# Silu in one function, squares and a rounded copy behind it, and norm sums in two parts, in the convolution of a fused two-layer kernel

## What is computed

```python
gqkv = jax.nn.silu(causal_conv(gqkv, conv_w)).astype(f32)
gq, gk, gv = jnp.split(gqkv, [GDN_HEADS * GDN_DK, 2 * GDN_HEADS * GDN_DK], axis=-1)
gq = l2_normalize(gq.reshape(b, s, GDN_HEADS, GDN_DK)) * (GDN_DK ** -0.5)
gk = l2_normalize(gk.reshape(b, s, GDN_HEADS, GDN_DK))
gv = gv.reshape(b, s, GDN_HEADS, GDN_DV)
...
def l2_normalize(t):
    return t * lax.rsqrt(jnp.sum(t * t, axis=-1, keepdims=True) + 1e-6)
```

## Time and profile before

| | |
|---|---|
| median of 3 runs | 2767.71 us (2766.85 to 2773.09) |
| profiled execution | 2766.82 us, its span 2765.1 us |
| TensorE clock granted | 1.00 of full over the span |
| TensorE matmuls, weight loads | 2746.5 us, 2443.9 us busy |
| VectorE, ScalarE, GpSimd | 1907.3, 1353.2, 59.4 us busy |
| stage of the delta rule beside convolutions | about 1055 to 1580 us |

### The profile page before, as it was taken

One profiled execution on the slowest core, in us unless ns is written; L12 is line 12 of the kernel. 1 busy time (PEld: TensorE's weight loads), 2 busy tenths in 40 slices (PEclk: granted clock), 3 DMA queues, 4 the chain that ended last, 5 costly groups with the idle time before them and its releaser, 6 DMA issues.

```text
span 2765.1 us, 39573 instructions
## 1 busy us (share of the span) xinstructions
PE 2746.5 (99%) x16256; PEld 2443.9 (88%) x16256; DVE 1907.3 (69%) x2553; ACT 1353.2 (49%) x1741; POOL 59.4 (2%) x103
## 2 busy tenths in 40 slices
PE   9999999999999999999999999999999999999998
PEld 8899888888888889999999988888888888888887
DVE  7655567778866657888888885566666655666556
ACT  5434654447444436656565643543354443444444
POOL 0000210000000000000000000000000000000000
PEclk9999999999999999999999999999999999999999
DMA  7444445465555454444444445554355455555554
GB/s 273 183 193 158 151 169 197 184 251 184 208 178 211 180 186 168 153 153 153 151 154 151 169 168 212 183 191 163 141 206 197 184 192 204 202 194 191 195 193 152
DMA packets 72852, 506.64 MB, mean 183 GB/s; under 512 B 8384, under 2 KB 8512, under 8 KB 12896
## 3 DMA queue, kind: packets, MB, share of 16 engines
q1 hardware_dynamic: 71136, 497.77, 48.6%
q0 software_dynamic: 1104, 5.90, 0.6%
q10 hardware_dynamic: 432, 0.45, 0.0%
HBM read 499.89 MB, written 2.10 MB: 182 GB/s over the span
## 4 chain that ended last, share of the span: by engine, by line
PE 95%; DVE 3%; ACT 1%; issue 1%; DMA 1%; SPq 0%; DVEq 0%; ACTq 0%
PE double L1399 88%; PE bank L1399 6%; PE bank L1402 1%; DVE wlo L2117 1%; ACT whi L1775 0%; DVE AA L2123 0%; DMA vec<-in_vec 0%; DMA raw<-in_wall 0%; DVE Tn L2625 0%; DVE gz L2117 0%; ACT tmp L1952 0%; DVE ob L2123 0%; DVE acc L2117 0%; ACT L1952 0%; SPq L2920 0%
## 5 line engine op out<-in xcount | busy, mean ns | idle before, releaser
L1399 PE MATMUL double<-AA,whi 128*128 128x512 f32 (+3 forms) x5776 | 1617.0, 348 | 3.3 <-DVE wlo L2117 3.2
L1775 ACT ACTIVATE whi<-raw 128x1024 fp32r<-128x1024 f32 x926 | 926.1, 1050 | 785.2 <-PE double L1399 735.1
L1399 PE MATMUL double<-AA,wlo 128*128 128x256 f32 (+1 forms) x4624 | 1274.9, 276 | 0.0
L2117 DVE TENSOR_TENSOR wlo<-raw,whi 128x1024 fp32r<-128x1024 f32 (+1 forms) x934 | 1100.4, 1214 | 191.8 <-ACT whi L1775 188.7
L1399 PEld LDWEIGHTS double<-AA,whi 128*128 128x128 f32 (+1 forms) x5776 | 1003.9, 188 | 147.3 <-DVE wlo L2117 5.0
L1399 PEld LDWEIGHTS double<-AA,wlo 128*128 128x128 f32 x4624 | 866.7, 187 | 1.0
L1399 PE MATMUL double<-whi,AA 128*128 128x512 f32 x1536 | 481.0, 388 | 0.0
L1399 PEld LDWEIGHTS double<-whi,AA 128*128 128x128 f32 x1536 | 288.1, 188 | 52.7 <-issue 1.9
L1399 PE MATMUL double<-whi,BB 128*128 128x512 f32 x1024 | 309.5, 382 | 0.0
L1399 PE MATMUL double<-wlo,AA 128*128 128x512 f32 x768 | 293.4, 382 | 0.0
L1399 PEld LDWEIGHTS double<-whi,BB 128*128 128x128 f32 x1024 | 191.8, 187 | 33.8
(11 more groups left out here) (334 smaller groups left out, 1688.1 us busy)
## 6 DMA issues: line engine op xcount, KB each, us to landing
raw<-in_wall SPq DMA_DIRECT2D x462, 1024.0 KB, 4.8
raw<-in_wall SPq DMA_DIRECT2D x9, 256.0 KB, 6.4
X<-in_xT SPq DMA_DIRECT2D x1, 2048.0 KB, 11.3
Mm<-in_memT POOLq DMA_DIRECT2D x1, 2048.0 KB, 15.5
tmp<-rqk POOLq DMA_DIRECT2D x16, 128.0 KB, 2.2
mblk<-in_memT SPq DMA_DIRECT2D x8, 256.0 KB, 4.5
dec<-in_dec POOLq DMA_DIRECT2D x1, 1536.0 KB, 8.6
hs<-in_hsT SPq DMA_DIRECT2D x4, 272.0 KB, 5.6
```

The lines of the kernel that those rows point to most:

```text
L1399: return q.matmul(out, lhsT, rhs, start=start, stop=stop, skip_group_check=True)
L1775: q.activation(hi_of(j)[:, c], raw[j % RAW][:, c], ACT.Copy).then_inc(S("w_hi"), 1)
L2117: return q.tensor_tensor(out, a, b, o)
```

## The change

For q, k and v ScalarE applies Silu to `cacc` and writes `qkv[n]` itself; the product on VectorE goes away. For q and k two more functions follow at once on ScalarE: the square into the temporary buffer, and a copy of it rounded to fp32r into `cacc_r`, which lies where `cacc` lies. VectorE then subtracts the rounded copy from the square (stage `cvl`, in the place of `cvq`), and the sum over partitions is two fp32r matmuls with a matrix of ones rounded to fp32r: one of the high part, one of the low. The next convolution's first tap waits for these two matmuls, since they read the place of `cacc`; after v's it waits for Silu. v's convolution takes no temporary buffer. `ones_r` is written once, by ScalarE, at the start of the stage.

```diff
 g_conv:
         r = add("cv1", (h, n), v=up("cnv_vec", 4))
+        if n == 2:
+            r = add("cvs", (h, n), a=up("cnv_act"))
+            P.cacc = P.at["got", ("v", h)] = ("cnv_act", r["a"])
+            tasks.append(g_gdn(h))
+            return
         t, tf = tmp.take()
         tmp.held.add(t)
-        r = add("cvs", (h, n), t=t, tf=tf, a=up("cnv_act"))
-        if n == 2:
-            tasks.append(g_gdn(h))
-            yield
-            r = add("cvv", h, t=t, z=up("cnv_vec"))
-            tmp.free(t, "cnv_vec", r["z"])
-            P.cacc = ("cnv_vec", r["z"])
-            P.at["got", ("v", h)] = ("cnv_vec", r["z"])
-            return
+        r = add("cvs", (h, n), t=t, tf=tf, a=up("cnv_act", 3))
         yield
         if h:
             lo_to(done["lo"] + 1)
-        r = add("cvq", (h, n), t=t, z=up("cnv_vec"), a=up("cnv_act"))
-        P.cacc = ("cnv_vec", r["z"])
+        r = add("cvl", (h, n), t=t, lo=up("cnv_vec"))
         yield
         yield
         b, bf = side.take()
         r = add("cvn", (h, n), t=t, b=b, bf=bf, full=up("cnv_pe"), a=up("cnv_act", 2))
         side.free(b, "cnv_act", r["a"] - 1)
+        P.cacc = ("cnv_pe", r["full"])
...
+    cacc_r = place(kpos[1], [P_, 512], F32R, name="cacc_r")
+    ones_r = place(con_off + 4 * CON["room"][0], [P_, P_], F32R, name="ones_r")
...
 TensorE, s_cvn:
-            q.wait_ge(S("cnv_act"), at["cvq", key]["a"])
-            mm_group(bank[r["b"]][:, :], C("ones"), tmps[r["t"]][:, :]).then_inc(S("cnv_pe"), 1)
+            q.wait_ge(S("ones_r"), 1)
+            q.wait_ge(S("cnv_act"), at["cvs", key]["a"])
+            mm_group(bank[r["b"]][:, :], ones_r[:, :], cacc_r[:, :], start=True, stop=False)
+            q.wait_ge(S("cnv_vec"), at["cvl", key]["lo"])
+            mm_group(bank[r["b"]][:, :], ones_r[:, :], tmps_r[r["t"]][:, :], start=False, stop=True).then_inc(S("cnv_pe"), 1)
...
 ScalarE:
+        def s_begin_gdn(_, r):
+            q.wait_ge(S("ret_m"), RET_END)
+            q.activation(ones_r[:, :], C("ones"), ACT.Copy).then_inc(S("ones_r"), 1)
+
         def s_cvs(key, r):
-            q.preload_act_table_set("sigmoid_and_others")
-            free(r["tf"])
+            h, n = key
+            q.preload_act_table_set("silu_and_others")
+            if h:
+                q.wait_ge(S("gdn_pe"), at["g_vb" if n == 2 else "g_x", h - 1]["p"])
             q.wait_ge(S("cnv_vec"), at["cv1", key]["v"])
-            q.activation(tmps[r["t"]][:, :], f2(cacc), ACT.Sigmoid).then_inc(S("cnv_act"), 1)
-
-        def s_cvq(key, r):
-            q.wait_ge(S("cnv_vec"), r["z"])
-            s = tmps[r["t"]][:, :]
-            q.activation(s, f2(qkv[key[1]]), ACT.Square).then_inc(S("cnv_act"), 1)
+            q.activation(f2(qkv[n]), f2(cacc), ACT.Silu).then_inc(S("cnv_act"), 1)
+            if n < 2:
+                s = tmps[r["t"]][:, :]
+                free(r["tf"])
+                q.wait_ge(S("cnv_act"), r["a"] - 2)
+                q.activation(s, f2(qkv[n]), ACT.Square).then_inc(S("cnv_act"), 1)
+                q.wait_ge(S("cnv_act"), r["a"] - 1)
+                q.activation(cacc_r[:, :], s, ACT.Copy).then_inc(S("cnv_act"), 1)
...
 VectorE:
-        def s_cvq(key, r):
-            h, n = key
-            if h:
-                q.wait_ge(S("gdn_pe"), at["g_x", h - 1]["p"])
+        def s_cvl(key, r):
             q.wait_ge(S("cnv_act"), at["cvs", key]["a"])
-            tt(f2(qkv[n]), f2(cacc), tmps[r["t"]][:, :], ALU.mult).then_inc(S("cnv_vec"), 1)
+            tt(tmps_r[r["t"]][:, :], tmps[r["t"]][:, :], cacc_r[:, :].bitcast(F32), ALU.subtract).then_inc(S("cnv_vec"), 1)
```

More of the change, by code:

```diff
@@ L105 @@
 for _name, _n in (("ident", 128), ("ones", 128), ("nones", 128), ("ntri", 128), ("upto", 128), ("beyond", 128),
-                  ("strict", 64), ("eye", 64), ("below", 64), ("m2", 32), ("m4", 32), ("m8", 32),
+                  ("strict", 64), ("room", 128), ("eye", 64), ("below", 64), ("m2", 32), ("m4", 32), ("m8", 32),
                   ("m16", 32), ("m32", 32), ("invf", 1), ("eps6", 1), ("eps5", 1), ("eps12", 1), ("sgn", 1), ("mhalf", 4)):
@@ L120, in constants @@
         "upto": p <= f, "beyond": p > f, "strict": g < r, "below": -1.0 * ((g == r) | ((r % 2 == 1) & (g == r - 1))),
-        "eye": p % 64 == f[:, 0:64], "mhalf": np.full((P, 4), -0.5), "sgn": np.where(np.arange(P) < 64, -1.0, 1.0)[:, None],
+        "eye": p % 64 == f[:, 0:64], "room": np.zeros((P, P)), "mhalf": np.full((P, 4), -0.5), "sgn": np.where(np.arange(P) < 64, -1.0, 1.0)[:, None],
         "invf": (1.0 / (np.float32(10000.0) ** (np.arange(0, 128, 2, dtype=np.float32) / np.float32(128))))[
@@ L2100, in scalar_program @@
                "a7": gained("a7", lambda k: V("norm_ffn_g_2", k)), "trig": s_trig, "gab1": s_gab1, "gab2": s_gab2, "rg_sig": token_sigmoid(lambda h, m: Gt[h % 2][:, m, :]),
-               "gta_sig": token_sigmoid(None), "rtr": s_rtr, "rav": s_rav, "cvs": s_cvs, "cvq": s_cvq, "cvn": s_cvn,
+               "gta_sig": token_sigmoid(None), "rtr": s_rtr, "rav": s_rav, "begin_gdn": s_begin_gdn, "cvs": s_cvs, "cvn": s_cvn,
                "gz_sig": token_sigmoid(lambda h, m: gz[m][:, :]), "gtb_sig": token_sigmoid(None), "g_dec": s_g_dec, "g_inv0": s_g_inv0, "g_down": s_g_down,
@@ L2570, in s_cv1 @@
             last_cv[0] = r["v"]
-        def s_cvv(h, r):
-            if h:
-                q.wait_ge(S("gdn_pe"), at["g_vb", h - 1]["p"])
-            q.wait_ge(S("cnv_act"), at["cvs", (h, 2)]["a"])
-            tt(f2(qkv[2]), f2(cacc), tmps[r["t"]][:, :], ALU.mult).then_inc(S("cnv_vec"), 1)
-        def s_cvq(key, r):
-            h, n = key
-            if h:
-                q.wait_ge(S("gdn_pe"), at["g_x", h - 1]["p"])
+        def s_cvl(key, r):
             q.wait_ge(S("cnv_act"), at["cvs", key]["a"])
-            tt(f2(qkv[n]), f2(cacc), tmps[r["t"]][:, :], ALU.mult).then_inc(S("cnv_vec"), 1)
+            tt(tmps_r[r["t"]][:, :], tmps[r["t"]][:, :], cacc_r[:, :].bitcast(F32), ALU.subtract).then_inc(S("cnv_vec"), 1)
         def s_cvy(key, r):
@@ L2842, in vector_program @@
                "rsc": s_rsc, "rav": s_rav, "rn": s_rn, "begin_gdn": s_begin_gdn, "conv": s_conv, "cv0": s_cv0,
-               "cv1": s_cv1, "cvv": s_cvv, "cvq": s_cvq, "cvy": s_cvy, "gz": s_gz,
+               "cv1": s_cv1, "cvl": s_cvl, "cvy": s_cvy, "gz": s_gz,
                "gz_in": gate_on(gdn_gate, None, "gz"), "gtb": s_token_gate, "gtb_in": gate_on(gdn_gate, "gz_in", "gtb"), "g_dec": s_g_dec,
@@ L2933, in s_load_mb @@
         def s_load_mb(n, r):
-            name, value = (("cnv_vec", at["cv1", (7, 2)]["v"]), ("cnv_vec", at["cvv", 7]["z"]), ("gdn_act", at["g_dec", 7]["x"]),
+            name, value = (("cnv_vec", at["cv1", (7, 2)]["v"]), ("cnv_act", at["cvs", (7, 2)]["a"]), ("gdn_act", at["g_dec", 7]["x"]),
                            ("gdn_vec", at["g_mat", 7]["w"]), ("gdn_pe", at["g_x", 7]["p"]), ("gdn_pe", at["g_vb", 7]["p"]),
```

## The result

The changed kernel takes 2774.0 us in the median of 18 runs (2772.72 to 2778.97); beside it the kernel before takes 2767.55 (2765.48 to 2773.39, 18 runs). The ratio is 1.0024, 95% interval 1.0018 to 1.003. It is slower by 0.24%, just over the bound of 0.2% (the interval reaches down to 0.18%), and 2.0 us above the forecast of 2772.0. The profiled execution took 2773.14 us, its span 2771.4.

The account below looks back on a forecast made before the run. TensorE, 99% busy and locked to VectorE once per head, bounds the kernel. Head 0 gives -0.78 us, seven heads at +0.72 give +5.04: total +4.3, predicted 2772.0 us, range 2765 to 2778.

Parts of the forecast that it names:

- case A: Convolution stage: TensorE delayed through VectorE, +0.65 to +0.9 us per head; chance 0.57, of which 0.47 within 0.2%.
- sign of being wrong: Profile after: g_v's load not 0.12 us behind VectorE's copy, shrinking head period, over 1.0 us added per head, new table loads.
- The pair saves 0.39 and only nine sums count: Norm sums on TensorE: 0.47 us for 0.86; savings count for both of head 0 and k's of seven heads.
- Three functions ahead of the roundings, TT 0.73 late: ScalarE at q: Silu, Square, Copy precede the weight roundings, delaying the previous head's inverse evacuation TT by 0.73 us.
- k's subtraction waits 0.38: VectorE at k: subtraction waits 0.38 us for ScalarE's Copy, delaying the copy of TT that TensorE's g_v needs.
- The roundings 1.3 us later cost nothing: ScalarE's weight roundings come 1.32 us later but are made units ahead of their use: 0.
- VectorE's multiplications give nothing: VectorE: sixteen products become equal subtractions; v's eight go, 0.60 us each, but the waits that follow hide the gain: 0.
- VectorE's wait before vb takes up what is left: VectorE after g_v: its 1.26 us wait before vb absorbs 0.39 us of extra lateness, so no more builds up.
- B: Whole stage: delays are absorbed and the saving stands, 6.2 us gained, 2761.5 us; chance 0.13.
- B': Stage: only one of the two delays, TT's or the subtraction's, reaches TensorE; about 2767 to 2769 us; chance 0.07.
- C: Norm sums: the plain-order fp32r pair is no quicker than the fp32 matmul; +7.8 us, 2775.5; chance 0.20.
- D: ScalarE: Square or Copy not in Silu's set, each taking another table load; about 18 us, 2790; chance 0.03.

Follow-up runs that it names:

- pair_only: Kernel before, with the square rounded to fp32r and the sum as two fp32r matmuls of that high part, no low part; 2764.52 us, ratio 0.999.
- mix_late: Changed kernel with k's subtraction behind VectorE's copy of TT; q has Silu, square behind TT's evacuation, fp32 sum; 2765.87 us, again 2763.84.
- q_only: Changed kernel with k's convolution in the old form, q's and v's in the new; 2773.18 us, ratio 1.0021 against the kernel before.
- q_new_k_late: Changed kernel with only k's subtraction moved one slot later, behind VectorE's copy of TT; 2769.39 us, ratio 1.0006 against the kernel before.
- q_sqlate_k_new: Changed kernel, but q has only Silu, its square behind TT's evacuation and an fp32 sum; 2764.82 us, ratio 0.9984 against the kernel before.
- k_only: Changed kernel with q's convolution in the old form, k's and v's in the new; 2772.14 us, ratio 1.0011 against the kernel before.
- fp32_sum: Changed kernel with the sum as one fp32 matmul again, rounded copy and subtraction still made; 2777.82 us, ratio 1.0039 against the kernel before.
- silu_only: Kernel before with Silu replacing sigmoid and product for q, k, v; square at its old place, fp32 sums; 2769.34 us, ratio 1.0001.
- two_func: Changed kernel without Copy and subtraction: Square writes rounded fp32r, low part left out; 2765.36 us, ratio 0.9987 against the kernel before.

## Why the prediction was right

Its case A came in, in sign, place and mechanism, but over a third larger than worked out: +5.9 us in the stage for +4.3. By the measured prices heads 1 to 7 lose 0.94 us each, for 0.72. The head's period grew by 1.0 us to 70.2, where 69.9 was forecast, and that is the very edge of the prediction's own sign of being wrong (more than 1.0 us). It had given 0.54 to a time within 0.2% and 0.10 to A beyond it; the 0.24% is the less likely of the two, by a narrow margin.

- *The pair saves 0.39 and only nine sums count:* right (0.38 in head 3, and pair_only's 3.6 us).
- *Three functions ahead of the roundings, TT 0.73 late:* mis-sized; this is the larger of the two terms that were too small. It measured 0.87. I had each dependent function 0.03 us behind the one before; Silu to Square is 0.09, because the wait for the buffer is an instruction there (0.06). And from 0.68 and 0.77 I took the middle, as if TT might overlap the roundings. It starts 0.02 us after their end (1268.07 + 2.00, TT at 1270.09), and the way from the roundings to TT is 0.52 shorter without the square, not 0.55.
- *k's subtraction waits 0.38:* it measured 0.46. 0.06 is that wait again. The idle time in the profile shows only 0.37 of it. The low half behind the subtraction starts 0.08 us before the subtraction's end (1283.02 + 0.69, then 1283.63), as an instruction does that needn't wait; one that waits loses that overlap.
- These two make 7 x (0.14 + 0.08) = 1.5 of the 1.6 us that were missing.
- *The roundings 1.3 us later cost nothing:* right; the view of waits has no such wait, and in mix_late k's are so late and no load of the projection waits for them.
- *VectorE's multiplications give nothing:* right for the changed kernel, where a subtraction took their place. Not so as a rule: without q's and k's the stage is 1.55 us shorter. The prediction had seen the load of g_v bound to the copy, and did not ask what the instruction in between was worth.
- *VectorE's wait before vb takes up what is left:* right, 0.88 for 1.26.
- *cacc_r in cacc's place costs nothing:* the view of waits shows no tap waiting for it; it was not undone by itself.
- *Table loads as many:* right. The rate of the new function, too: Silu takes 0.63.
- The rule of back-to-back functions overlapping by 0.09 us (the Trainium skill, ScalarE: Activation LUTs, "What ACT_TABLE_LOAD costs") would have given +0.8 us. The dependent functions show +0.03 and +0.09, so the measurement stands against using it for them; the independent roundings behind Copy do start 0.09 ahead of its end (1267.53 + 0.63, then 1268.07).
- Rivals: B falls by q_only and by the load rows. B' falls because either delay alone reaches TensorE (q_only and q_new_k_late have TT's alone, q_sqlate_k_new and k_only the subtraction's). C falls by pair_only and fp32_sum, D by the table loads, which are 24 as before.

## What to carry to other kernels

When an engine that seems free takes over work, count what stands behind it in its queue, and follow that to the engine that bounds: two functions put ahead of one small evacuation, and a subtraction that waits for them, cost more than the quicker sums saved. k's subtraction one slot later, behind what others wait for, took 5.1 us off again. Find such locks by the starts of weight loads against the ends of their producers, since a busy share of 99% does not show them.

## What was not expected of the hardware

- A second wait ahead of a ScalarE function costs 0.06 us: Silu to Square 0.72 with it, 0.67 without it, in all sixteen places of either kernel.
- Executions of one kernel can fall at two levels. Of the changed kernel's 18, eleven lie in 2772.7 to 2774.7 us and seven in 2777.8 to 2779.0, and nothing between; silu_only and two_func show no such gap. In profiles of the upper level (q_only, k_only, fp32_sum) TensorE is 5 to 6 us behind the trace before at 1012 us, where it was within 0.7 at 679 us, in a part of the program that no kernel here changes. Its cause stays open.
